# Routing of the first tile and the samples placed ahead of the last output product, and the last tile's row split moved from VectorE to GpSimd and ScalarE

## The reference

```python
x = x + merged @ w_out                       # 264 rows in tiles of 128, 128 and 8
h = rmsnorm(x, norm_ffn)
logits = h @ w_router + b_router             # 32 experts
top_vals, top_idx = lax.top_k(logits, 4)
gates = jax.nn.softmax(top_vals, axis=-1)
x = x + sum over the 4 picked experts of gate * swiglu_expert(h)
```

## Time and profile before

| what | value |
|---|---|
| median of three runs | 1353.21 us (1349.29 to 1357.77) |
| the profiled execution, its own time | 1350.02 us |
| its span, first to last instruction | 1348.2 us |
| PE busy / DVE / ACT / POOL | 95% / 29% / 17% / 5% of the span |
| DMA moved | 516.96 MB, mean 383 GB/s |
| mixer and seam / experts and end | 0 to 418 us / 418 to 1348 us |

### The profile page before, as it was taken

How to read it: one execution, slowest core, us unless ns; L and a number is a source line. 1 busy time by engine, 2 the same in 40 slices (tenths; PEclk the granted TensorE clock), 3 DMA queues, 4 the chain that set the end, 5 groups by cost and what they waited for, 6 DMA issues and landing times.

```text
span 1348.2 us, 18792 instructions
## 1 busy us (share of the span) xinstructions
PE 1276.2 (95%) x7701; PEld 636.6 (47%) x7701; DVE 386.3 (29%) x865; ACT 227.8 (17%) x369; POOL 61.1 (5%) x104
## 2 busy tenths in 40 slices
PE   6999888999997999999999999999999999999998
PEld 5675477778643434343444433334433333433334
DVE  3004764522225222232222222222222222222222
ACT  2011122211232111111111111111111111111112
POOL 2003512200000000000000000000000000000000
PEclk9999999999998999999999999999999999999999
DMA  9999987778975999999999999999999999999994
GB/s 334 390 340 342 325 289 262 254 270 314 385 297 211 415 427 428 428 428 428 428 429 429 428 428 428 428 429 428 429 429 429 428 428 429 428 428 428 429 429 202
DMA packets 57567, 516.96 MB, mean 383 GB/s; under 512 B 5615, under 2 KB 6855, under 8 KB 32160
## 3 DMA queue, kind: packets, MB, share of 16 engines
q1 hardware_dynamic: 50000, 493.68, 89.0%
q0 software_dynamic: 7344, 22.62, 5.2%
q10 hardware_dynamic: 192, 0.23, 0.1%
HBM read 512.98 MB, written 49.87 MB: 417 GB/s over the span
## 4 chain that ended last, share of the span: by engine, by line
PE 61%; DMA 30%; DVE 5%; issue 2%; ACT 1%; POOL 0%; SPq 0%; DVEq 0%; ACTq 0%; POOLq 0%
PE psum L580 58%; DMA weights<-in_w_gate_up 26%; PE psum L583 3%; DMA rel_copies<-rel_rows 2%; DVE spatial L1428 1%; DMA weights<-in_w_mem_kv 1%; DMA weights<-in_cache_mem_kv 1%; DVE late L1271 0%; DVE kvt L1018 0%; DVE x L1307 0%; DVE weights L1122 0%; DVE memory L1325 0%; DVE va L1143 0%; DVE va L1144 0%; ACT late L1581 0%
## 5 line engine op out<-in xcount | busy, mean ns | idle before, releaser
L580 PE MATMUL psum<-weights,spatial 128*64 128x512 f32 x1536 | 358.2, 599 | 19.6 <-DMA weights<-in_w_gate_up 18.0
L1397 DVE TENSOR_TENSOR hT<-psum,hT 128x264 f32<-128x264 f32 x256 | 92.9, 426 | 485.4 <-PE psum L580 485.4
L580 PE MATMUL psum<-weights,merged 128*64 128x512 f32 (+2 forms) x896 | 218.1, 595 | 0.0
L580 PEld LDWEIGHTS psum<-weights,spatial 128*64 128x64 f32 x1536 | 103.0, 136 | 211.9 <-issue 166.5
L580 PE MATMUL psum<-hT,weights 128*128 128x264 f32 x704 | 165.4, 392 | 1.2 <-DVE late L1271 0.9
L580 PEld LDWEIGHTS psum<-hT,weights 128*128 128x128 f32 x704 | 134.4, 193 | 28.9 <-DVE late L1271 4.5
L580 PEld LDWEIGHTS psum<-weights,merged 128*64 128x64 f32 (+2 forms) x896 | 72.3, 141 | 122.6 <-issue 120.3
L1637 ACT COPY bT<-psum 128x264 f32<-128x264 f32 x33 | 12.5, 378 | 473.2 <-PE psum L583 473.2
L1428 DVE TENSOR_SCALAR spatial<-psum,lowest 128x512 f32<-128x512 f32 x64 | 48.1, 751 | 148.9 <-PE psum L580 145.5
L580 PE MATMUL psum<-bT,merged 64*128 64x264 f32 x512 | 74.3, 409 | 0.0
L580 PEld LDWEIGHTS psum<-bT,merged 64*128 64x128 f32 x512 | 44.1, 186 | 55.6 <-issue 51.9
(11 more groups left out here) (286 smaller groups left out, 859.8 us busy)
## 6 DMA issues: line engine op xcount, KB each, us to landing
weights<-in_w_gate_up SPq DMA_DIRECT2D x96, 2048.0 KB, 32.4
weights<-in_w_down SPq DMA_DIRECT2D x48, 2048.0 KB, 34.0
memory<-in_w_gate_up SPq DMA_DIRECT2D x16, 2048.0 KB, 32.4
late<-in_w_gate_up SPq DMA_DIRECT2D x16, 2048.0 KB, 33.9
out<-in_cache_win_kv SPq DMA_DIRECT2D x8, 4094.0 KB, 23.2
weights<-in_w_in SPq DMA_DIRECT2D x13, 2048.0 KB, 13.8
late<-in_w_down SPq DMA_DIRECT2D x8, 2048.0 KB, 33.0
memory<-in_w_down SPq DMA_DIRECT2D x8, 2048.0 KB, 33.6
```

The costliest lines, as they stand in the source:

```text
L580: return nc.tensor.matmul(out, lhsT, rhs, start=start, stop=stop, **kw)
L1397: V.tensor_tensor(acc[:, c, :], p_a[j % 2][part], acc[:, c, :], ALU.add).then_inc(s_acc, 1)
```

## The change

The list of the seam is written anew. Tile 0's transposes and the samples' come right behind the samples' second product, then `scale 0` and the splits of tile 0 and the samples; after `wo 1 0` come the router product `rt 0` and the logits and choices `lg 0` of tile 0 and the samples; `wo 1 1` follows, then the same for tile 1 alone. `rt` and `lg` have two parts each. `rt 0` is copied out by VectorE, `rt 1` by ScalarE. Inside `lg 0` TensorE already does the first two of the eight k steps of `wo 1 1`, into the bank of that later step, and waits for that bank first. The max and index of max move from `top` to `lg`. For tile 1, GpSimd makes the normed rows (into `h_tok`), subtracts the high part and later the middle part; ScalarE casts `h_tok` to the middle part; VectorE has no part in it. GpSimd's zeroing of `y_tok` and its two DMA issues wait for `wo 1 1` in place of `rt` and stand ahead of its three new instructions. `count_over` goes ahead of the gate weights.

```diff
-    s += [("wos", 0), ("wos", 1), ("wo", 0, 0), ("woz", 0), ("wo", 0, 1), ("woz", 1), ("scale", 0), ("hi", 2), ("hi", 0)]
-    s += [("wo", 1, 0), ("xt", 2, 0), ("xt", 0, 0), ("rest", 2), ("wo", 1, 1), ("xt", 0, 1), ("xt", 1, 0), ("scale", 1), ("xt", 1, 1)]
-    s += [("rest", 0), ("hi", 1), ("lo", 2), ("lo", 0), ("rt",), ("rest", 1), ("lg",), ("top",), ("pos",)]
+    s += [("wos", 0), ("wos", 1), ("wo", 0, 0), ("woz", 0), ("wo", 0, 1), ("woz", 1), ("xt", 0, 0), ("xt", 0, 1), ("xt", 2, 0)]
+    s += [("scale", 0), ("hi", 2), ("hi", 0), ("rest", 2), ("rest", 0), ("lo", 2), ("lo", 0), ("wo", 1, 0), ("rt", 0), ("lg", 0), ("wo", 1, 1)]
+    s += [("xt", 1, 0), ("xt", 1, 1), ("scale", 1), ("rt", 1), ("hi", 1), ("lg", 1), ("rest", 1), ("top",), ("pos",)]
...
-        lgT = bT_all[:, 0:NT]
+        lgT = th[0]
...
-            pool.wait_ge(s_job, job[("rt",)] + 1)
+            pool.wait_ge(s_job, job[("wo", 1, 1)] + 1)
             nc.gpsimd.memset(y_tok, 0.0).then_inc(s_yzero, 1)
...
+            pool.wait_ge(s_scale, 2)
+            nc.gpsimd.tensor_scalar(h_tok, x1[:, 1, :], stat[:, 24 + NORMED[1]:25 + NORMED[1]], None, ALU.mult).then_inc(s_xnorm, 1)
+            pool.wait_ge(s_xnorm, 1)
+            pool.wait_ge(s_xhi, 3)
+            nc.gpsimd.tensor_tensor(h_tok, h_tok, xparts[:, 0, 1, :], ALU.subtract).then_inc(s_xrest, 1)
+            pool.wait_ge(s_xmid, 3)
+            nc.gpsimd.tensor_tensor(xparts[:, 2, 1, :], h_tok, xparts[:, 1, 1, :], ALU.subtract).then_inc(s_xlo, 1)
...
-                    last = row_tile(o, merged, weights(f"o{n}"), t, 512)
+                    last = row_tile(o, merged, weights(f"o{n}"), t, 512, range(2 if (t, n) == (1, 1) else 0, KD))
...
                 elif kind == "rt":
+                    part, = a
                     pe.wait_ge(s_router, 1)
...
+                    taken(pe, *(("xt", 2, 0) if part == 0 else ("xt", 1, 0)))
+                    for seg, (t0, tn) in enumerate((TILES[0], TILES[2]) if part == 0 else (TILES[1],)):
+                        for k in range(KD):
+                            if k == 4:
+                                taken(pe, "xt", part, 1)
...
                 elif kind == "lg":
-                    taken(pe, "rt")
-                    for t, (t0, tn) in enumerate(TILES):
-                        last = mm(o[0:tn, t * E:(t + 1) * E], lgT[:, t0:t0 + tn], quarters)
+                    part, = a
+                    if part == 0:
+                        follower = job[("wo", 1, 1)]
+                        pe.wait_ge(s_taken[follower % 3], follower // 3)
+                        row_tile(bank[follower % 3], merged, weights("o1"), 1, 512, range(2))
+                    taken(pe, "rt", part)
+                    for t, at in ((0, 0), (2, P)) if part == 0 else ((1, P + NS),):
...
                 elif kind == "rest":
                     t, = a
+                    if t == 1:
+                        continue
...
+                elif kind == "rt" and a[0] == 0:
+                    ready()
+                    V.tensor_copy(lgT[:, 0:P + NS], o[:, 0:P + NS]).then_inc(free, 1)
...
-                elif kind == "top":
-
-                    for t in range(3):
+                    for t in ts:
                         seq(V.max(mx8[:, t, :], lg[:, t, :]))
                         seq(V.max_index(idx[:, t, :], mx8[:, t, :], lg[:, t, :]))
+                elif kind == "top":
...
                 if isinstance(b, int):
-                    low_part(1)
+                    count_over()
                     gate_weights()
                 take_x(b * (E + 1))
-                if isinstance(b, int):
-                    count_over()
...
-                    A.copy(xparts[0:tn, 1, t, :], x1[0:tn, t, :]).then_inc(s_xmid, 1)
-                elif kind == "rt":
+                    A.copy(xparts[0:tn, 1, t, :], h_tok if t == 1 else x1[0:tn, t, :]).then_inc(s_xmid, 1)
+                elif kind == "rt" and a[0] == 1:
                     act.wait_ge(s_job, n + 1)
-                    A.copy(lgT[:], o[:, 0:NT]).then_inc(free, 1)
+                    A.copy(lgT[:, P + NS:NT], o[:, 0:P]).then_inc(free, 1)
```

More of the change, by code:

```diff
@@ L372, in build @@
         s_scale, s_xhi, s_xrest, s_xmid, s_xlo = (sem("rows_" + n) for n in ("scale", "high", "rest", "mid", "low"))
-        s_router, s_grows_in = sem("router_gained"), sem("in_gain_by_row_pair")
+        s_xnorm, s_router, s_grows_in = sem("rows_normed"), sem("router_gained"), sem("in_gain_by_row_pair")
         s_iota = sem("iota")
@@ L597, in wide_tile, with row_tile @@
                 return last
-            def row_tile(out, lhs, w, t, n):
+            def row_tile(out, lhs, w, t, n, ks=range(KD)):
                 t0, tn = TILES[t]
-                for k in range(KD):
+                for k in ks:
                     last = mm(out[0:tn, 0:n], lhs[:, k, t0:t0 + tn], w[:, k, 0:n], k == 0, k == KD - 1)
@@ L842, in _ @@
                 elif kind == "rt":
+                    part, = a
                     pe.wait_ge(s_router, 1)
[L844 to L851, removed]
-                elif kind == "lg":
-                    taken(pe, "rt")
-                    for t, (t0, tn) in enumerate(TILES):
-                        last = mm(o[0:tn, t * E:(t + 1) * E], lgT[:, t0:t0 + tn], quarters)
+                    taken(pe, *(("xt", 2, 0) if part == 0 else ("xt", 1, 0)))
[3 more added lines that the diff above has]
+                                taken(pe, "xt", part, 1)
+                            r = slice(k % 4 * E, (k % 4 + 1) * E)
+                            last = mm(o[r, seg * P:seg * P + tn], wr[:, k, :], rowsT[:, k, t0:t0 + tn], k < 4, k >= 4)
+                elif kind == "lg":
+                    part, = a
[5 more added lines that the diff above has]
+                    for t, at in ((0, 0), (2, P)) if part == 0 else ((1, P + NS),):
+                        tn = TILES[t][1]
+                        last = mm(o[0:tn, t * E:(t + 1) * E], lgT[:, at:at + tn], quarters)
                 elif kind == "pos":
@@ L1328, in _ @@
                         V.tensor_tensor(bias[2 * E:3 * E, 0:2 * D], brow, flat_qk.bitcast(BF16)[0:E, 0:2 * D], ALU.subtract).then_inc(s_bias, 1)
+                elif kind == "rt" and a[0] == 0:
+                    ready()
+                    V.tensor_copy(lgT[:, 0:P + NS], o[:, 0:P + NS]).then_inc(free, 1)
                 elif kind == "lg":
+                    part, = a
                     ready()
                     dve.wait_ge(s_grows_in, 16)
-                    dve.wait_ge(s_scale, 2)
-                    for t, (_, tn) in enumerate(TILES):
+                    dve.wait_ge(s_scale, part + 1)
+                    ts = (0, 2) if part == 0 else (1,)
+                    for t in ts:
+                        tn = TILES[t][1]
                         ins = V.scalar_tensor_tensor(lg[0:tn, t, :], o[0:tn, t * E:(t + 1) * E], stat[0:tn, 24 + NORMED[t]:25 + NORMED[t]],
                                                      br[0:tn, :], ALU.mult, ALU.add)
-                        if t < 2:
+                        if t != ts[-1]:
                             seq(ins)
```

## The result

The changed kernel takes 1363.75 us (median of 11 runs, 1360.14 to 1374.33); the kernel before took 1352.88 us beside it. The ratio is 1.0078, with a 95% interval of 1.006 to 1.0097: about 10.9 us slower, where the prediction had 1.0 us faster and a range that ended at 1358.

What follows compares the result with a forecast made beforehand. Bound: the saturated weight stream, so expert 0's start sets the end. Last product's addition 4.1 us later, stretch behind it 5.1 us shorter: 1.0 us earlier, 1353.2 - 1.0 = 1352.2 us; range 1347 to 1358.

Steps and rivals of the forecast that it cites:

- Scaling to 3.4: GpSimd's scaling for tile 1 starts with the scale (2.3), takes 1.05 us, ends 3.4 us behind the last product's addition.
- A quarter of the last product (1.8 us): First part of `wo 1 1` on TensorE, after the wait for VectorE's addition: 1.8 us, to 398.6.
- 3.7 us: Time from expert 0's start until it has used up its first ring slot and chunk 8 is issued.
- The low clock at expert 0: Rival: clock rises a step later, expert 0's first 3.7 us could take twice that; 2.7 us later in all; chance 0.07.
- Slow GpSimd: Rival: each new GpSimd instruction takes 5.2 us, the gather's last matmuls wait; expert 0 starts 7.0 us later; chance 0.10.
- The held VectorE: Rival: VectorE's two-SBUF-input instructions (comparison, mask) wait for GpSimd's subtractions; expert 0 starts 2.4 us later; chance 0.33.
- The undelayed product: Rival: quicker splits let TensorE resume at the end of `rt 0`; 1.5 to 2.8 us gained in all; chance 0.05.
- the likeliest case alone: The forecast without rivals, chance 0.42: -1.4 to +0.2 us on its sum, some 4 us median scatter; 1347.5 to 1356.5.

Runs made afterwards that it cites:

- E1: Kernel before, with scalings and subtractions of a spare tile put on idle GpSimd, ahead of and behind its all-reduce; 1357.68 us, one run.
- E2: Changed kernel with one small scaling and one subtraction on GpSimd 160 us ahead of the seam; 1354.94 us, 1.0009 to before.
- E3: Changed kernel with tile 1's rest and low part given back to VectorE, new list order kept; 1356.75 us, 1.0023 to before.
- E4: Changed kernel with `wo 1 0` and `rt 0` moved ahead of the two low parts in the list; 1364.35 us, 1.0068 to before.
- E5: Changed kernel with the edits of E2 and E4 together; 1352.81 us, 0.9991 to before.
- E9: E5 with GpSimd's second subtraction given to VectorE behind the selection; 1352.23 us, 0.9991 to before.
- E11: Kernel before with an extra all-reduce of 128x8 ones on GpSimd some 35 us ahead of its own; 1351.56 us, 0.9985 to before.
- E12: E10 plus the early all-reduce of E11; 1351.77 us, 0.9988 to before.
- E7: E6 plus nine unread TensorE products, seven ahead of the counting of rows, two behind it; 1352.02 us, 0.9987 to before.
- E8: Kernel before plus nine unread TensorE products, seven ahead of the counting of rows, two behind it; 1355.69 us, 1.0009 to before.
- E10: E6 plus twelve unread TensorE products spread over idle places from the last product to expert 0; 1349.39 us, 0.9977 to before.
- E6: Changed kernel with the edits of E3 and E4 together; 1356.56 us, 1.0015 to before.

## Why the prediction was wrong

**What held.** The end hangs on expert 0's start and the weight stream: the rest of the span behind chunk 8 is the same within 0.5 us before and after. TensorE's resumption at the bank of `wo 1 1` was put at 12.66 us behind the samples' second sum and came at 12.61 (400.65 - 388.04), and the wait named there was the wait seen, only longer (2.24 in place of about 1 us, since `rt 0` took 0.75). Behind the addition the comparison stands at 4.48 (4.65 predicted), the gather at 7.77 (7.9). The subtractions take 2.12 us (2.1 predicted), but by luck: the 2.1 was twice the price of one input, taken from the memset, and the scaling, which has one input, took 2.85 us and not 1.05.

**What failed, by size.** The sum was 1.0 us earlier, the stretch came out 13.7 later; 14.7 us are missing.

- *"Scaling to 3.4"*, which took for granted that GpSimd starts when the scale is there. It began 11.6 behind the addition in place of 2.3 (9.3 us) and took 2.85 us in place of 1.05 (1.8); 0.9 of that was spare, since the first subtraction was to wait for the high part until 4.3. E1 and E2 show the first as the change from the all-reduce to plain arithmetic. The prediction quoted the row that holds the same thing: its all-reduce row ends in 11.66 us of idle time with "issue" as releaser, and I read from it only the 0.81. The path from there on was right: the exponential stands behind the cast in ScalarE's queue, so the gate weights waited for GpSimd, as the sum had it. All told the stretch from addition to expert 0 is 23.09 in place of 12.6: 10.5 us.
- *"A quarter of the last product (1.8 us)"*. It took 3.65 at a clock that fell to 0.50 at the end of TensorE's 2.24 us of waiting: 1.8 us. The sum had the wait and no clock in it. E3 and E4 show the same quarter at 1.95 us, E3 with the same wait.
- *"3.7 us"* from expert 0's start to chunk 8. It took 6.19, at the low clock: 2.5 us.

The last two are of the clock, which differs between executions of the same instructions (E3, E1); the first is there in both runs that have GpSimd unprepared (9.85 us in the change, 9.86 in E4), and is gone in E2.

**The rivals.** The low clock at expert 0 came true, with 2.5 of its 3.7 us. Slow GpSimd had the right place, the gather waiting for tile 1's parts, and the wrong cause: apart from the scaling's 1.8 us the instructions were not slow, they began late. The held VectorE hardly appears in the change itself (0.43 us on the first gate-weight instruction, 429.47), because GpSimd came when VectorE had nothing to do; E2 and E5 show it at full price, 3.55 us, once GpSimd is on time, and E9 the mask's part of it, 1.74. In E2 and E5 the gather begins 11.32 us behind the addition and expert 0 15.37, near this rival's 11.7 and 16.0 and not the forecast's 7.9 and 12.6. Not all of it as stated: the held copies have one input, where the rival spoke of instructions with two. And the comparison, with two SBUF operands, was not held by the scaling, which reads SBUF as well. The measurement decides here against the wording of "Who interferes with whom" in the Trainium skill's "SBUF — State Buffer", where any GpSimd instruction that reads SBUF would have held it; with the mask beside the first subtraction the trace agrees. The undelayed product did not come: the wait for VectorE's addition was there.

The range of the likeliest case alone does not quite come out of its own figures: 1.4 us below to 0.2 above the 1353.2, with 4 us to either side, is 1347.8 to 1357.4 and not 1347.5 to 1356.5. The measured median lies outside both.

The change's 10.9 us in the medians and 13.7 in the profiled stretches do not contradict each other: the code of before has 3.69 us from expert 0's start to chunk 8 in two profiles (before, E11) and 6.07 in a third (E1), whose seam is the same, so a median of it holds some of the latter. The quarter of the last product adds 1.7 us of the same kind to the change's own executions (E3).

## What to carry to other kernels

Before work is given to an engine that has been idle, look at the idle time ahead of its first instructions, above all where the releaser is "issue", and ask whether its last work was of another kind; a small instruction of the new kind, issued while the engine has nothing to do, moved that time off the path here (E2). In a hand-written list, a product that waits for a bank waits for everything that the bank's reader has in front of it: E4 is one swap, and worth 4.1 us of the stretch, though its time does not show them. And a wait of TensorE can cost twice, once itself and once at the clock behind it (2.0 and 1.7 us); in E3 it cost only itself. So read the granted clock beside each stretch before a difference is put down to the change.

## What the runs showed that I had not expected

GpSimd's change between its all-reduce and plain arithmetic costs time in both directions: 7.9 to 9.9 us of idle time ahead of the first scaling, 8.3 to 8.6 ahead of the first all-reduce in E1, E11 and E12, and 11.0 to 11.7 in the others, whether the scores came early in that time (before: 0.8 us into the 11.66) or late (E4: 3.8 us into the 11.12). Why these differ was not tried. Its one-input scaling is slower than its two-input subtraction: 2.86 against 2.12 us for 1024 elements per partition, 1.25 against 0.83 for 384.

Filling idle time on TensorE kept the clock only when the products were spread: with nine in two places it fell all the same (E7, E8), with twelve in five places it stayed at 1.00 and the stretch was 2.2 us shorter than without them (E10 against E6).

Most of the scatter of the profiled executions lies ahead of the seam: in the fourteen profiles the samples' second sum starts between 383.7 and 392.5 us, while the rest of the span behind chunk 8 stays within 925.7 to 928.2. Why the mixer scatters was not tried.
